# Hybrid decoder layer on 8 cores: a new order of the first loads, and a shared shift-and-scale of blocks 2 and 3

## The reference, cut to what matters

```
mod = silu(c) @ w_ada + b_ada              -> shift, scale, gate (1024 each)
h   = RMSNorm(x) * norm_w * (1 + scale) + shift
u_A, v_A, z_A, q, k, v_B, z_B = h @ w_in   (7 groups of 512 columns)
A   = u_A * (tril(W_s) RMSNorm(v_A) + b) * silu(z_A)      in chunks of 128 positions
B   = RMSNorm((softmax(q1 k1) - lambda softmax(q2 k2)) v_B) * silu(z_B)   causal, 4 heads
out = x + gate * ([A | B] @ w_out)
```

## Time and profile before

| what | value |
|---|---|
| median of 3 runs (range) | 525.61 us (525.59 to 526.62) |
| the profiled execution's own time | 526.04 us |
| its span on the slowest core (core 4) | 524.6 us |
| spans of the 8 cores | 514.8 to 524.6 us |
| PE, DVE, ACT, POOL busy, share of the span | 85%, 64%, 57%, 17% |
| DMA, mean over the span | 103 GB/s |

### The profile page before, as it was taken

How to read it: one execution, slowest core, us unless ns; L and a number is a source line. 1 busy time by engine, 2 the same in 40 slices (tenths; PEclk the granted TensorE clock), 3 DMA queues, 4 the chain that set the end, 5 groups by cost and what they waited for, 6 DMA issues and landing times.

```text
span 524.6 us, 9798 instructions; the slowest of 8 cores (514.8 to 524.6 us)
## 1 busy us (share of the span) xinstructions
PE 445.6 (85%) x3104; PEld 217.6 (41%) x3104; DVE 334.7 (64%) x761; ACT 299.2 (57%) x402; POOL 88.6 (17%) x118
## 2 busy tenths in 40 slices
PE   0037679899999999999998999979997999999396
PEld 0002224344443444444445555445554555555242
DVE  1246732682775468888873767788558757868732
ACT  1066456545554227777767666666778778677100
POOL 1113440000671000000001112222222222122100
PEclk9997869899999999999999999979998999999879
DMA  8999978007624300021021122194140131011013
GB/s 200 251 308 257 311 240 180 0 1 131 167 87 139 121 1 2 1 47 36 1 81 41 42 81 60 62 282 202 47 156 2 39 100 67 22 62 42 40 63 139
DMA packets 15606, 53.90 MB, mean 103 GB/s; under 512 B 2242, under 2 KB 2626, under 8 KB 14660
## 3 DMA queue, kind: packets, MB, share of 16 engines
q1 hardware_dynamic: 13924, 45.36, 26.0%
q0 software_dynamic: 1152, 7.50, 8.3%
q10 hardware_dynamic: 480, 0.41, 0.3%
HBM read 50.29 MB, written 8.39 MB: 112 GB/s over the span
## 4 chain that ended last, share of the span: by engine, by line
PE 60%; DVE 11%; DMA 9%; issue 7%; ACT 6%; POOL 5%; DVEq 0%; SPq 0%; ACTq 0%; POOLq 0%
PE psum L647 15%; PE psum L470 13%; PE psum L1049 8%; PE psum L927 7%; DMA sb_WO<-w_adaT 5%; PE psum L897 5%; ACT sb_cs L910 3%; DMA sb_kT<-xT 3%; PE psum L1015 3%; POOL sb_cs L915 3%; DVE sb_F L984 3%; DVE sb_F L943 1%; PE psum L677 1%; PE psum L675 1%; PE psum L667 1%
## 5 line engine op out<-in xcount | busy, mean ns | idle before, releaser
L910 ACT ACTIVATE sb_cs<-psum,sb_small 128x1024 bf16<-128x1024 f32 x144 | 150.9, 1113 | 58.6 <-PE psum L897 55.2
L927 PE MATMUL psum<-sb_vB,sb_cs 128*128 128x129 bf16 x1088 | 89.5, 226 | 9.7 <-DVE sb_F L943 5.2
L927 PEld LDWEIGHTS psum<-sb_vB,sb_cs 128*128 128x128 bf16 x1088 | 64.4, 100 | 40.5 <-issue 40.1
L470 PE MATMUL psum<-sb_W,sb_hT 128*128 128x512 bf16 x256 | 65.8, 420 | 17.5 <-ACT sb_hT L466 15.4
L915 POOL TENSOR_TENSOR sb_cs<-sb_cs,sb_constb 128x256 bf16<-128x256 bf16 x64 | 44.5, 697 | 213.3 <-ACT sb_cs L910 208.7
L647 PE MATMUL psum<-sb_hT,sb_W 128*128 128x512 bf16 x280 | 65.8, 379 | 0.0
L897 PE MATMUL psum<-sb_qT,sb_kT 64*128 64x256 bf16 (+1 forms) x576 | 56.4, 274 | 6.9 <-ACT sb_cs L910 4.7
L470 PEld LDWEIGHTS psum<-sb_W,sb_hT 128*128 128x128 bf16 x256 | 26.4, 105 | 56.2 <-issue 34.1
L357 DVE SCALAR_TENSOR_TENSOR sb_F<-sb_WO,sb_F 128x1024 f32<-128x1024 f32 x24 | 30.2, 1257 | 30.5 <-DMA sb_WO<-w_adaT 22.0
L647 PEld LDWEIGHTS psum<-sb_hT,sb_W 128*128 128x128 bf16 x280 | 27.3, 98 | 30.0
L436 PE MATMUL psum<-sb_vnA,sb_constb 128*128 128x512 bf16 x32 | 11.9, 507 | 30.5 <-ACT sb_vnA L429 30.5
(11 more groups left out here) (114 smaller groups left out, 548.4 us busy)
## 6 DMA issues: line engine op xcount, KB each, us to landing
sb_WO<-w_adaT SPq DMA_DIRECT2D x24, 512.0 KB, 8.1
sb_W<-w_in POOLq DMA_DIRECT2D x5, 1024.0 KB, 9.9
sb_W<-x SPq DMA_DIRECT2D x8, 512.0 KB, 4.4
sb_cs<-w_out SPq DMA_DIRECT2D x8, 512.0 KB, 3.4
sb_hT<-x SPq DMA_DIRECT2D x8, 512.0 KB, 12.0
out<-sb_hT SPq DMA_DIRECT2D x8, 512.0 KB, 2.6
out<-sb_W SPq DMA_DIRECT2D x6, 512.0 KB, 2.8
sb_qT<-xT SPq DMA_DIRECT2D x4, 512.0 KB, 23.4
```

Source lines behind the costliest of these rows:

```text
L470: pe(lambda E: E.matmul(PS(bank), lhsT=hT[:, kc, 128 * tt:128 * (tt + 1)], rhs=wsl[slot][:, kc, :], start=(kc == 0), stop=(kc == KC - 1)), ...
L910: act(lambda E: E.activation(out=et, in_=psum[:, X:X + 2, :], func=AF.Exp, bias=negM, scale=0.125), reads=[pb[X], pb[Y], b_lam], writes=[b ...
L927: pe(lambda E, u=u, j=j, c=c, i=i: E.matmul(psum[:, j, 256 * c:256 * c + 129], lhsT=et[:, c, QB * u + 128 * j:QB * u + 128 * (j + 1)], rhs ...
```

## The change

The first loads are issued in another order. Block 0 of x leads SP's queue, then come c, the first four blocks of `w_ada`, and all of block 1. The v_B weights wait until block 0 has landed, and the constants of POOL's queue follow them. The matrix of ones for the row sums is written on chip by DVE. The z_B weights are issued after the products of the start and wait for the 14th block of `w_ada`. SiLU of c runs after block 0's norm. `mod_kc` becomes two operations on DVE. The products of block 1 start after those of chunk 4 of block 0. In blocks 2 and 3, every second chunk is scaled and shifted on ACT, and the steps are spread between the z_B tiles.

```diff
@@ -370,15 +370,18 @@
     for qt in range(4):
         P.dma("act", posc[32 * qt:32 * (qt + 1), :], pos1[512 * qt:512 * (qt + 1)].partition_broadcast(32),
               b_pos[qt], writes=[b_pos[qt]])
+    load_xT(0)
     P.dma("sp", c_bc, c_d.rearrange("a n -> (a n)").partition_broadcast(128), b_F[0], writes=b_c)
-    P.dma("pool", constb[:, :], cb_d, b_constb, writes=[b_constb])
     ADA = []
     for kc in range(KC):
         ADA += [kc, 8 + kc]
-    for j in ADA[0:4]:
-        load_ada(j, (0, 1, 2, 3))
-    load_xT(0)
-    load_w(0, G_VB)
+    ada_dma = [load_ada(j, (0, 1, 2, 3)) for j in ADA[0:4]]
+    load_w(0, G_VB, extra=[x_last[0]])
+    P.dma("pool", constb[:, :], cb_d, b_constb, writes=[b_constb])
+    load_xT(1)
+    ones_t = sb("ones_t", [128, 128], BF16)
+    b_ones = buf("ones_t")
+    dve(lambda E: E.memset(ones_t[:, :], 1.0), writes=[b_ones])
 
     dve(lambda E: E.memset(epsn, NORM_EPS), writes=[b_sc])
     dve(lambda E: E.memset(epss, SUBLN_EPS), writes=[b_sc])
@@ -433,8 +436,8 @@
     def phaseMM(tb, q):
         bank = 6 + tb % 2
         for kc in (2 * q, 2 * q + 1):
-            pe(lambda E, kc=kc: E.matmul(PS(bank), lhsT=ones_b, rhs=sqx[tb % 2][:, kc, :], start=(kc == 0), stop=(kc == KC - 1)),
-               reads=[b_constb, b_vn[8 * (tb % 2) + kc]], writes=[pb[bank]])
+            pe(lambda E, kc=kc: E.matmul(PS(bank), lhsT=ones_t[:, :], rhs=sqx[tb % 2][:, kc, :], start=(kc == 0), stop=(kc == KC - 1)),
+               reads=[b_ones, b_vn[8 * (tb % 2) + kc]], writes=[pb[bank]])
 
     def phaseLn(tb):
         bank = 6 + tb % 2
@@ -475,7 +478,6 @@
         act(lambda E: E.activation(out=vB[:, tt, :, 0:128], in_=PS(bank).rearrange("p (h d) -> p h d", h=4), func=AF.Copy),
             reads=[pb[bank]], writes=[b_vB[tt]])
 
-    act(lambda E: E.activation(out=c_bc, in_=c_bc, func=AF.Silu), reads=b_c, writes=b_c)
     pool(lambda E: E.tensor_scalar(out=bada1, in0=bada[:, 8:16], scalar1=1.0, scalar2=None, op0=ALU.add),
          reads=[b_small], writes=[b_bada1])
     pool(lambda E: E.tensor_scalar(out=swcol, in0=swcol, scalar1=1.0 - LAM_INIT, scalar2=None, op0=ALU.mult),
@@ -484,15 +486,19 @@
     def mv(n):
         matvec(ADA[n])
         if n + 4 < 16:
-            load_ada(ADA[n + 4], (0, 1, 2, 3))
+            ada_dma.append(load_ada(ADA[n + 4], (0, 1, 2, 3)))
 
     def mod_kc(kc):
-        pool(lambda E: E.tensor_tensor(out=shift[:, kc:kc + 1], in0=modraw[:, kc:kc + 1], in1=bada[:, kc:kc + 1], op=ALU.add),
-             reads=[b_small, b_raw_[kc]], writes=[b_mod[kc]])
-        pool(lambda E: E.tensor_tensor(out=gvec[:, kc:kc + 1], in0=modraw[:, 8 + kc:9 + kc], in1=bada1[:, kc:kc + 1], op=ALU.add),
-             reads=[b_bada1, b_raw_[8 + kc]], writes=[b_mod[kc]])
-        pool(lambda E: E.tensor_tensor(out=gvec[:, kc:kc + 1], in0=gvec[:, kc:kc + 1], in1=normw[:, kc:kc + 1], op=ALU.mult),
-             reads=[b_small, b_mod[kc]], writes=[b_mod[kc]])
+        dve(lambda E: E.tensor_tensor(out=shift[:, kc:kc + 1], in0=modraw[:, kc:kc + 1], in1=bada[:, kc:kc + 1], op=ALU.add),
+            reads=[b_small, b_raw_[kc]], writes=[b_mod[kc]])
+        dve(lambda E: E.scalar_tensor_tensor(out=gvec[:, kc:kc + 1], in0=modraw[:, 8 + kc:9 + kc], scalar=bada1[:, kc:kc + 1],
+                                             in1=normw[:, kc:kc + 1], op0=ALU.add, op1=ALU.mult),
+            reads=[b_bada1, b_small, b_raw_[8 + kc]], writes=[b_mod[kc]])
+
+    def pair(kc):
+        mv(2 * kc)
+        mv(2 * kc + 1)
+        mod_kc(kc)
 
     def start_mm(tb, kc):
         phaseB(tb, kc, "act")
@@ -500,37 +506,36 @@
             vb_main(tt, tt % 8, kc)
 
     phaseA(0)
-    mv(0)
-    mv(1)
-    load_xT(1, (0, 1))
-    mv(2)
-    mv(3)
-    load_xT(1, (2, 3))
-    mv(4)
-    mv(5)
+    act(lambda E: E.activation(out=c_bc, in_=c_bc, func=AF.Silu), reads=b_c, writes=b_c)
+    phaseM(0, 0)
+    phaseM(0, 1)
+    pair(0)
+    start_mm(0, 0)
+    phaseM(0, 2)
+    phaseM(0, 3)
+    pair(1)
+    start_mm(0, 1)
+    phaseA(1)
+    pair(2)
+    start_mm(0, 2)
+    pair(3)
+    start_mm(0, 3)
+    phaseM(1, 0)
+    phaseM(1, 1)
+    pair(4)
+    start_mm(0, 4)
     for kc in range(3):
-        mod_kc(kc)
-    for q in range(4):
-        phaseM(0, q)
-    for kc in range(2):
+        start_mm(1, kc)
+    phaseM(1, 2)
+    phaseM(1, 3)
+    for kc in range(5, 8):
+        pair(kc)
         start_mm(0, kc)
-    phaseA(1)
-    start_mm(0, 2)
-    for i in range(5):
-        kc = 3 + i
-        mv(2 * kc)
-        mv(2 * kc + 1)
-        mod_kc(kc)
-        if i < 4:
-            phaseM(1, i)
-        start_mm(0, kc)
-        for k1 in ((0, 1), (2, 3), (4, 5), (6,), (7,))[i]:
+        for k1 in ((3, 4), (5, 6), (7,))[kc - 5]:
             start_mm(1, k1)
-        if i == 0:
-            load_w(1, G_ZB)
-        if i == 4:
-            for tt in range(4):
-                vb_evac(tt, tt)
+    for tt in range(4):
+        vb_evac(tt, tt)
+    load_w(1, G_ZB, extra=[ada_dma[13]])
     load_xT(2)
     load_xT(3)
     for s_ in (0, 1):
@@ -728,11 +733,10 @@
         dve(lambda E: E.tensor_scalar(out=nlam, in0=nlam, scalar1=-LAM_INIT, scalar2=None, op0=ALU.add),
             reads=[b_lam], writes=[b_lam])
 
-    def prepB(tb):
-        for q in range(4):
-            phaseM(tb, q)
-            phaseB(tb, 2 * q, "dve")
-            phaseB(tb, 2 * q + 1, "dve")
+    def prepB(tb, q):
+        phaseM(tb, q)
+        phaseB(tb, 2 * q, "dve")
+        phaseB(tb, 2 * q + 1, "act")
 
     def zb(tt):
         step(make_tile(G_ZB, tt, 1))
@@ -745,13 +749,11 @@
     for q in range(4):
         phaseMM(2, q)
     phaseLn(2)
-    prepB(2)
-    zb(5)
-    phaseSq(3, 0)
-    zb(6)
-    phaseSq(3, 1)
-    zb(7)
-    phaseSq(3, 2)
+    prepB(2, 0)
+    for q in range(3):
+        zb(5 + q)
+        prepB(2, q + 1)
+        phaseSq(3, q)
     drain()
     phaseSq(3, 3)
     for kc in range(KC):
@@ -761,9 +763,12 @@
             for q in range(4):
                 phaseMM(3, q)
             phaseLn(3)
-    prepB(3)
+    prepB(3, 0)
+    prepB(3, 1)
     for tt in range(8, 12):
         vb_evac(tt, tt % 4)
+    prepB(3, 2)
+    prepB(3, 3)
     for kc in range(KC):
         for tt in range(12, 16):
             vb_main(tt, 4 + tt % 4, kc)
```

## The result

The changed kernel takes 532.84 us (median of 4 runs, 532.31 to 534.22), beside 525.6 us (524.91 to 526.62) before. The ratio is 1.014, with a 95% interval of 1.0106 to 1.0173: 7.2 us slower. Slower was the likelier side of the prediction, but the value was 527.0 and the range ended at 531.5. In some executions of most kernels, the one before too, the cores of a die ran at a lower clock and the time was 3% or more longer; all ratios here leave these out.

The account below looks back on a forecast made before the run. The start was taken as bound by loads, then the last chunk's `shift` and `gvec`; the rest by PE. Core 7: 523.1 - 2.0 + 5.3 = 526.4, + 1.44 = 527.8, less 0.43 and 0.4: 527.0 us, range 522 to 531.5.

Parts of the forecast that it names:

- Part 2: Blocks 2 and 3: ScalarE's added scalings delay SiLU and copies that PE needs; 4.7 plus 0.6, together 5.3 us slower.
- M2: Landmark: start of block 2's 8 ones-products, right after zb(4); forecast 76.3 us on core 4, 77.4 on core 7.
- The sign that I gave: Block 2: PE waits for four SiLUs, zb(7)'s 13.7 us behind the Ln's table load instead of 8.9.
- The "free" rival: Blocks 2 and 3: their change costs nothing because PE is behind ACT there; 521.7 us, chance 0.08.
- The chain of VectorE: Start: matrix-vector products set the pace from weight 7 at about 44.5 us; last `gvec` at 63.4, products end at 67.9.
- The z_B weights are a second path to zb(0): Start: z_B load issued behind weight 13 at 54.7 us, takes 13.2, lands at 67.9, level with the products' end.
- that gap: Start: the four slots leave queue q1 open for a microsecond or two, as weight 14 is issued once weight 13 has landed.
- The starved z_B load: Start: the z_B issue on POOL is held up 4 to 5 us beside busy VectorE; time 532, chance 0.12.
- The winning start: Start: transfers keep 0.322 MB/us, weight 7 at 39 to 41, everything behind 4 us earlier; time 523.4, chance 0.35.
- The reference point: After M2: core 7 needs 443.6 us to its end, core 4 441.4, so core 7 sets the time; 0.4 taken off.

Follow-up runs that it names:

- e4: The kernel before with only blocks 2 and 3 changed: second chunks scaled on ScalarE, steps spread between the z_B tiles; ratio 1.0111 to the kernel before.
- e2: The changed kernel with the z_B weights waiting for weight block 15, the last, instead of 13; ratio 1.0258 to the kernel before.
- e1: The changed kernel with the z_B weights waiting for weight block 7 instead of 13; ratio 1.0104 to the kernel before.
- e3: The changed kernel with blocks 2 and 3 prepared as before, all chunks scaled on VectorE; ratio 1.0096 to the kernel before.
- e5: The changed kernel again, without an edit, on a second chip; ratio 1.0156 to the kernel before.
- e6: The changed kernel with z_B weights waiting for weight block 7 and blocks 2 and 3 prepared as before; ratio 0.999 to the kernel before.
- e9: The kernel before with shift and scale as two VectorE operations and the z_B load bound to weight block 7; ratio 0.998 to the kernel before.

## Why the prediction was right and wrong

**Part 2 was right, in place and size.** Forecast 4.7 us at zb(7)'s SiLU and 0.6 at the copy of tile 8. Measured from M2 to M3: 17.64 in the mean of eight cores against 12.84, that is 4.8, and 0.53 to 0.74 us of waiting for the copy. The sign that I gave, the end of zb(7)'s SiLU 13.7 us behind the Ln's table load, came as 13.3. The "free" rival, 0.08, fell with e4.

**The chain of VectorE was right.** Product 7 was put at 44.5; it started between 42.9 and 45.9 on the eight cores. From there the steps held, a little too slow: a pair with its small operations took 2.88 us (57.80 to 60.68 on core 6, products 12 to 14) where I had 3.13, so the small operations cost 0.2 a pair in my sum and not 0.45. Product 14 started at 60.68 on core 6. In e2, where nothing disturbs it, product 15 starts between 59.1 and 63.8, around the 61.7 that my last `gvec` at 63.4 implies.

**The step that failed is "The z_B weights are a second path to zb(0)".** I priced that load only for its own landing. I used its 54.5% of the engines to bound its own duration and never charged the other side. The rows had the price: beside that load q1 moved 1.75 MB in 13 us, 0.13 MB/us, against 0.322 alone. What q1 carried now was weight 15, on which the whole start hangs. The text even placed the z_B issue at 54.7 and weight 14's just after it, and then let the products run on to 63.4 as if alone. By my pace weight 15 lands 1.70 us behind weight 14; it landed 13.4 us after its issue on core 6, and 3.9 to 6.0 after it in e2 without the z_B load beside it. On six cores (0, 2, 3, 4, 6 and 7) product 15 waited 5.9 to 9.2 us; on cores 1 and 5 weight 15 got through in 5.4 us (waits of 0.4 and 0.85), and PE waited 6.6 and 6.4 for the z_B weights. Both ways M2 came 4.4 us (core 4) to 7.8 us (core 7) after my value. The mean rates do not explain 13.4 us for half a megabyte. On the six cores weight 15 landed within about 1.3 us of the z_B load, before or behind it; which of the two gets through first when they are issued within a microsecond of each other, and why, is not shown.

Three smaller terms went the same way. The z_B load took 16.7 us on core 1, not 13.2. The DMA engines stood empty for 1 us just ahead of it; I had named that gap and charged it to block 2 alone. And PE is slow after its long wait: the 40 products of zb(0) to zb(4) took 83.46 - 73.52 = 9.9 us on core 1, where I had 8.4. The rows of core 1 from the end of that wait on (window, its length, busy time of PE, PEld, DVE, ACT and POOL, granted clock, DMA share, GB/s):

```profile
73.50:75.50 2.00, 1.98 (x5) 0.71 (x6) 1.77 (x2) 0.00 (x0) 0.00 (x0) 0.50 1.02 348
...
75.50:83.40 7.90, 7.90 (x36) 3.50 (x35) 3.04 (x3) 3.56 (x5) 0.00 (x0) 0.95 0.86 336
```

After 6.57 us without a product the granted clock is 0.50 for the first 2 us, the lower of its two levels, and 0.95 in the mean of the rest. A term for this stood nowhere in my sum, and by e1 it is a good part of what the late load costs: the 48 products took 11.9 to 13.4 us in one piece on the cores of the changed kernel, e3 and e5, and 10.52 in e1.

**The rivals.** The starved z_B load (0.12) named the right load and the right result, 532, by a wrong mechanism: it was to be held up on POOL by DVE. The POOL instruction took 0.59 us here; the transfer was long, not its issue. That the time agreed was luck. The winning start (0.35) was not there: no core had product 7 before 42.9, and e6, with both losses gone, is at 0.999. The gain of the small operations (e9) was small: 0.2% in the time, at the edge of its interval.

**The reference point.** That core 7 was slow behind M2 was of one execution: 443.6 us from M2 to the end before, 445.3 after with 5.4 us added by part 2 up to M3, so 3.7 less without it.

## What to carry to other kernels

Where a load that the critical path hangs on is in flight, charge every other load that is issued beside it to that path, not only to its own user. Here the large load cost its neighbours something wherever it stood: 3.9 us of product 14 behind weight 7, and behind weight 13 a wait of 5.9 to 9.2 us for one weight, or of 6.4 to 6.6 us for the load itself. A stall also costs more than its length, since TensorE came back from it at a lower clock (48 products in 12.98 us after 9.21 us of waiting, 10.52 after 0.64). Before work is moved to the engine with the lower busy share, look at whose result another engine waits for in that stretch; ScalarE was at 57% of the span, and its added instructions between two SiLUs went into TensorE's idle time. And when operations are taken out of a queue, ask what they held back there: a load without a wait of its own moved from 44 us to 8.

## What the runs showed of the hardware

A load that converts float32 to bfloat16 on POOL's queue held 52.7 to 54.5% of the 16 DMA engines while 1.05 MB of it landed, and a 512 KB transfer of the SP queue beside it took 10.6 to 13.4 us from issue to landing on six cores (5.4 on the other two), where e2, without it, has 3.9 to 6.0. Its packets were few (144 beside 378), so one packet each in turn does not describe the sharing. The distance M3 - M2 was 17.5 us on every core of e1, e2, e4 and e5, with a granted clock between 0.76 and 0.85 in this stretch, so with ACT as the bound that clock hardly entered. In the changed kernel it was 17.7 to 17.9 on three cores, on which the ones-products that the Ln waits for took 2.06 or 2.27 us instead of 1.89. Without part 2 and with the squares in their old place it was 12.1 on the cores with a clock of 1.00, and 12.3 to 13.3 where the clock was 0.85 to 0.98. With the squares later PE had no wait in this stretch, and all 32 cores had 1.00 and 11.0 us. The converting load itself took 11.1 to 16.7 us in the changed kernel, and its share of the engines makes 7.1 to 7.4 us of all 16; why it takes so much longer, and which of the 16 engines finishes last, is left open.
